# A fused two-block network: the MLP's down-projection by seven products, and the output projection by token tile

## The reference

```python
h = rms_norm(x, norm_mix) * (1 + sc_m) + sh_m
y = fox_mixer(h, ...)              # attention; ends with o @ w_out
x = x + g_m * y
h = rms_norm(x, norm_mlp) * (1 + sc_f) + sh_f
x = x + g_f * (square(relu(h @ w_mlp_in)) @ w_mlp_out)   # 1024 -> 4096 -> 1024
```

## Time and profile before

| | |
|---|---|
| time of the launch, three runs | 3262.44 us median (3258.41 to 3263.48) |
| profiled execution: its time; its span | 3264.19 us; 3262.4 us |
| PE, DVE, ACT busy | 2970.6 (91%), 1293.9 (40%), 679.2 us (21%) |
| down-projection, L922 MATMUL x1024 | 446.0 us |
| output projection, L776 MATMUL x256 | 112.7 us |
| DMA over the span | 305.14 MB, 94 GB/s |

### The profile page before, as it was taken

How to read it: one execution, slowest core, us unless ns; L and a number is a source line. 1 busy time by engine, 2 the same in 40 slices (tenths; PEclk the granted TensorE clock), 3 DMA queues, 4 the chain that set the end, 5 groups by cost and what they waited for, 6 DMA issues and landing times. The chain is left out here.

```text
span 3262.4 us, 51362 instructions
## 1 busy us (share of the span) xinstructions
PE 2970.6 (91%) x20752; PEld 1924.7 (59%) x20752; DVE 1293.9 (40%) x3483; ACT 679.2 (21%) x1552; POOL 261.9 (8%) x343
## 2 busy tenths in 40 slices
PE   3999979988799999999998699999999989799996
PEld 2555546663488544886444377777777745444442
DVE  3222247761355201552001456666666537211115
ACT  2111146650200000000000134444444400111111
POOL 0000011100000000000000022222222200100001
PEclk9999989998899999999998899999999989799998
DMA  4011022211022320123213200000000020599974
GB/s 194 21 39 39 19 84 84 95 64 52 26 78 91 135 78 32 65 91 110 77 45 124 86 16 10 24 15 11 24 9 18 2 113 27 227 353 353 354 274 181
DMA packets 55409, 305.14 MB, mean 94 GB/s; under 512 B 6800, under 2 KB 8336, under 8 KB 39200
## 3 DMA queue, kind: packets, MB, share of 16 engines
q1 hardware_dynamic: 47248, 272.80, 22.8%
q0 software_dynamic: 6912, 25.17, 2.1%
q10 hardware_dynamic: 1040, 4.19, 0.3%
HBM read 269.04 MB, written 33.10 MB: 93 GB/s over the span
## 5 line engine op out<-in xcount | busy, mean ns | idle before, releaser
L922 PE MATMUL mlp_ps<-mlp_w2s,mlp_hid 128*128 128x512 f32 x1024 | 446.0, 599 | 7.4 <-DMA mlp_w2s<-in_w 7.4
L922 PEld LDWEIGHTS mlp_ps<-mlp_w2s,mlp_hid 128*128 128x128 f32 x1024 | 196.9, 193 | 255.3 <-issue 255.2
L328 PE MATMUL qkv_pq<-qkv_wq,h_hT 128*128 128x384 f32 x1024 | 330.5, 487 | 0.0
L1367 PE MATMUL rwkv_ps<-x_xT,rwkv_ws 128*128 128x256 f32 x1152 | 291.9, 391 | 0.0
L328 PEld LDWEIGHTS qkv_pq<-qkv_wq,h_hT 128*128 128x128 f32 x1024 | 194.8, 190 | 135.9 <-issue 0.9
L1367 PEld LDWEIGHTS rwkv_ps<-x_xT,rwkv_ws 128*128 128x128 f32 x1152 | 208.9, 191 | 28.9
L1037 DVE TENSOR_TENSOR mlp_small<-mlp_ps,b_gates 128x512 f32<-128x512 f32 x16 | 11.1, 691 | 421.1 <-PE mlp_ps L922 421.1
L1681 POOL TENSOR_TENSOR rwkv_ML<-rwkv_GM,rwkv_cst 128x256 f32<-128x256 f32 x120 | 99.9, 848 | 474.5 <-DVE rwkv_GM L1737 299.1
L966 ACT COPY mlp_first_copy<-mlp_ps 128x256 f32<-128x256 f32 x32 | 11.9, 372 | 599.7 <-PE mlp_ps L890 599.7
L890 PE MATMUL mlp_ps<-h_hT,mlp_w1s 128*128 128x256 f32 x512 | 122.9, 384 | 6.0 <-DMA mlp_w1s<-in_w 6.0
L1969 PE MATMUL mixr_ps<-mx_w_mix,mx_mixT 128*128 128x512 f32 x256 | 115.3, 606 | 8.7 <-DMA mixr_cnt<-in_counts 8.7
(11 more groups left out here) (382 smaller groups left out, 4593.9 us busy)
## 6 DMA issues: line engine op xcount, KB each, us to landing
mlp_w1s<-in_w SPq DMA_DIRECT2D x32, 1024.0 KB, 4.8
mlp_w2s<-in_w SPq DMA_DIRECT2D x64, 512.0 KB, 3.6
mx_gu<-in_w_gu SPq DMA_DIRECT2D x16, 2048.0 KB, 8.4
mx_w_mix<-in_w_gu SPq DMA_DIRECT2D x16, 2048.0 KB, 8.6
att_wa<-in_w_ada SPq DMA_DIRECT2D x32, 512.0 KB, 3.8
mx_dn<-in_w_d SPq DMA_DIRECT2D x16, 1024.0 KB, 10.3
mx_mixT<-in_w_d SPq DMA_DIRECT2D x16, 1024.0 KB, 10.5
y_rows<-ex_y SPq DMA_DIRECT2D x32, 512.0 KB, 3.0
```

The costliest lines, as they stand in the source:

```text
L328: last = nc.tensor.matmul(pq[:, b, 0:QN], lhsT=hT[:, k, t * P:(t + 1) * P], rhs=wq[:, n, k, :], start=(k == 0), stop=(k == KT - 1))
L922: return nc.tensor.matmul(ps[:, c, :], lhsT=hid[:, f, (c // 2) * P:(c // 2 + 1) * P], rhs=w2s[:, slot(f), (c % 2) * NB:(c % 2 + 1) * NB], ...
L1367: last = nc.tensor.matmul(ps[:, bank, 0:UT], lhsT=ws[:, n, k, :], rhs=xT[:, k, bass.ds(col, UT)], start=(k == 0), stop=(k == KT - 1))
```

## The change

**Output projection.** `stage_modulation_rest` goes, and its work moves into `stage_out`. `w_o` comes in eight DMAs of 512 KB during attention, each into the key columns of a head pair whose scores are done; its columns are laid out in pieces of 128 (512 bytes) for each row. PE makes the first gate, four token tiles (both halves of the width for each), the second gate and the column sums, and then the other four tiles.

**Down-projection.** For each half of the tokens there are two passes over `w2`, each for 256 tokens, with seven banks and seven products a pair of hidden tiles. DVE makes four sums of weights (T, 512 wide) and four of `hid` (S, 128 wide) for each pair, in `hT` columns that are no longer read, for two pairs in turn. ACT copies the seven results of a pass to SBUF, and DVE combines, scales and adds them in 15 steps (`finish`) beside the next pass or the next half's up-projection. `w2s` becomes four slots of two hidden tiles (1 MB), and all of `w2` is loaded four times instead of twice.

```diff
-def stage_modulation_rest(nc, ada_acc, b_ada, cols, modc, gates, ones):
...
@@ stage_attention, SP
+                    sp.wait_ge(maxed, 24 * (p - 1))
                     if p < HEAD_PAIRS:
-                        sp.wait_ge(maxed, 24 * (p - 1))
                         sp.dma_start(frow[:, p % 2, :, :], f_rows[2 * p:2 * p + 2, :].partition_broadcast(P)
                                      ).then_inc(f_in[p % 2], 16)
+                    sp.dma_start(qkv[:, :, cols(1, p - 2)], w_o[p - 2]).then_inc(wo_in, 16)
+                sp.wait_ge(wo_in, 16 * HEAD_PAIRS)
@@ stage_out, PE
+                gate_sums(0)
+                for t in range(TT):
+                    for n in range(2):
+                        m = 2 * t + n
                         if m >= 4:
                             pe.wait_ge(gated, m - 3)
                         for k in range(KT):
+                            last = nc.tensor.matmul(py[:, m % 4, :], lhsT=qkv[:, t, k * P:(k + 1) * P],
+                                                    rhs=qkv[:, k, D + n * NB:D + (n + 1) * NB], start=(k == 0), stop=(k == KT - 1))
                         last.then_inc(mm, 1)
+                    if t == 3:
+                        pe.wait_ge(gate_row, 1)
+                        gate_sums(1)
+                        column_sums(nc, ada_acc[1:3], pmod, ones).then_inc(mm_mod, 1)
@@ stage_mlp, PE: lhsT and rhs of the seven products of a pair, and a pass
+                    lhsT, rhs = {"m1": (raw(0, t1), weight(0, 0)), "m2": (raw(1, t1), weight(1, 0)),
+                                 "m3": (S[:, 3 * P:4 * P], weight(1, 1)), "m4": (raw(1, t2), T[2]),
+                                 "m5": (S[:, 0:P], T[0]), "m6": (S[:, P:2 * P], T[1]),
+                                 "m7": (S[:, 2 * P:3 * P], weight(0, 1))}[name]
...
+                    for i, name in enumerate(PRODUCTS):
...
+                        for j in range(2):
+                            down_product(g, j, name)
+                    for j in range(2, FPAIRS - 2):
+                        for name in PRODUCTS:
+                            down_product(g, j, name)
+                    for name in PRODUCTS:
+                        for j in range(FPAIRS - 2, FPAIRS):
+                            down_product(g, j, name)
@@ stage_mlp, ACT
+                    for g in range(2 * half, 2 * half + 2):
+                        for i in range(7):
+                            act.wait_ge(whole, 7 * g + i + 1)
+                            nc.scalar.copy(copies[g % 2][:, i, :], ps[:, i, :]).then_inc(copied, 1)
@@ stage_mlp, DVE: waits of a pair's sums, and what stands between two pairs
+                    if j >= 2:
+                        pair_done(dve, g, j - 2)
...
+                    pass_sums(2 * half, lambda: None)
+                    rest = finish(2 * half)
                     if half == 0:
+                        turned = tokens_of(1)
+                        pass_sums(1, lambda: (some(rest, 2), some(turned, 1)))
+                        every(sums_of(FPAIRS))
+                    else:
+                        pass_sums(3, lambda: some(rest, 2))
+                    rest = finish(2 * half + 1)
```

More of the change, by code:

```diff
@@ L826, in up_at @@
-        def up_at(j, name):
-            return 7 * j + PRODUCTS.index(name) + 1
-        def part_at(j, name):
-            return 7 * j + PARTS.index(name) + 1
-        def square_at(j, name):
-            return 4 * j + ("c22", "c11", "c21", "c12").index(name) + 1
-        def bank(j, name):
-            return (7 * j + PRODUCTS.index(name)) % 8
-        def slot(f):
-            return (f + 4) % G
+        summed, tokens, made, whole, copied, ended = (
+            s.sem(n) for n in "summed tokens made whole copied ended".split())
@@ new lines, in up_at, with part_at, square_at, bank @@
+        def up_at(n, name):
+            return 7 * n + PRODUCTS.index(name) + 1
+        def part_at(n, name):
+            return 7 * n + PARTS.index(name) + 1
+        def square_at(n, name):
+            return 4 * n + ("c22", "c11", "c21", "c12").index(name) + 1
+        def bank(n, name):
+            return (7 * n + PRODUCTS.index(name)) % 8
+        def slot(j):
+            return (j + 2) % 4
+        def made_order(g):
+            return ([(j, i, x) for i in range(4) for j in range(2) for x in "TS"] +
+                    [(j, i, x) for j in range(2, FPAIRS) for i in range(4) for x in "TS"])
@@ new lines, in pair_done @@
+        def pair_done(eng, g, j):
+            if j == FPAIRS - 1:
+                eng.wait_ge(whole, 7 * g + 7)
+            else:
+                eng.wait_ge(down, (FPAIRS - 1) * g + j + 1)
+        made_at = {}
+        for g in range(PASSES):
+            for key in made_order(g):
+                made_at[(g,) + key] = len(made_at) + 1
+        NEEDS = {"m5": ((0, "T"), (0, "S")), "m6": ((1, "T"), (1, "S")), "m7": ((2, "T"), (2, "S")),
+                 "m4": ((3, "T"),), "m3": ((3, "S"),)}
@@ L845, in pair_weights @@
                     n = half * FPAIRS + j
+                    if half and j < 2:
+                        sp.wait_ge(ended, 15)
                     if n >= 2:
@@ L943, in _ @@
[L943 to L958 removed]
+                    down_pass(2 * half)
@@ L1026, in gather @@
                     dve.wait_ge(squared, square_at(n, "c12"))
-                def take(half, c):
-                    m = half * 8 + c
-                    t, cs = half * 4 + c // 2, slice((c % 2) * NB, (c % 2 + 1) * NB)
-                    if c < 7:
-                        dve.wait_ge(whole, 7 * half + c + 1)
-                    else:
-                        dve.wait_ge(down, (half + 1) * FT)
-                    if m >= 2:
-                        dve.wait_ge(added, m - 1)
-                    nc.vector.tensor_tensor(tmp[:, m % 2, :], ps[:, c, :], gate[:, cs], ALU.mult).then_inc(gated, 1)
-                    dve.wait_ge(gated, m + 1)
-                    nc.vector.tensor_tensor(xres[:, t, cs], xres[:, t, cs], tmp[:, m % 2, :], ALU.add).then_inc(added, 1)
@@ L1043, in _, with some, pass_sums @@
+                def some(steps, count):
+                    for _ in range(count):
+                        next(steps, None)
+                def pass_sums(g, between):
+                    for key in made_order(g):
+                        down_sums(g, *key)
+                        if key[0] >= 2 and key[1:] == (3, "S"):
+                            between()
+                every(zip(tokens_of(0), sums_of(0)))
+                rest = iter(())
                 for half in range(2):
```

267 lines of the change are left out of this document (173 added, 94 removed).

## The result

| | before | after |
|---|---|---|
| time of the launch, median | 3262.78 us (3258.41 to 3263.48, four runs) | 3183.1 us (3179.2 to 3187.32, four runs) |
| ratio, 95% interval | | 0.9759 (0.9742 to 0.9776) |
| profiled execution: its time; its span | 3264.19; 3262.4 us | 3181.23; 3179.4 us |
| PE, DVE, ACT busy | 2970.6, 1293.9, 679.2 us | 2900.8, 1520.5, 696.2 us |
| DMA over the span | 305.14 MB, 94 GB/s | 338.75 MB, 107 GB/s |

A forecast was written before the change was run, and what follows sets the result against it. PE, busy for 91% of the span, was taken to bound the kernel. 68.5 + 16.7 - 1.0 - 1.0 - 3.7 = 79.5 us less gave 3183 us, range 3170 to 3198 us (forecast's own 3175 to 3190).

The forecast's parts named there:

- Products, waits for `w2`, and the clock behind them: Down-projections: 55.0 us less from 448 products instead of 512, 7.4 from waits, 6.1 from slow clock; 68.5 us less.
- rival of the second reading of `w2`: Down-projection: pairs 2 and 3 land 3 us late in each pass, 12 us more, 3195 us; chance 0.03.
- Start of each half: Down-projection, passes 1 and 3: PE waits about 0.5 us each for DVE's first sums; 1.0 us, between 0 and 3.
- DVE's pace: Down-projection: PE waits 1.0 us for DVE's sums, between 0 and 10; as a rival 3193 us, chance 0.07.
- slow steps: Down-projection: each 512-wide sum holds DVE 1.2 us, PE waits 37 us, 3220 us; chance 0.01.
- PE's waits: Down-projection: every semaphore wait costs PE 0.17 us, 65 us in all, 3248 us; chance 0.03.
- The end: End of the down-projection: DVE ends 5.1 us behind PE instead of 1.4; 3.7 us more, between 2 and 7.
- The output projection: PE's restart to the end of the output projection: 16.7 us less, between 10.5 and 18.
- the dip behind the column sums: Output projection: one-column products amid dense ones may make the clock fall; 1.3 us taken, between 0 and 3.1.
- the slow stretch at the start: Output projection: PE starts at half clock as before, costing 2.7 us both before and after the change.
- The loads of `w_o`: Attention: loading `w_o` there delays nothing on the path; 0 us, between 0 and 2.
- The clock as the way to a slower kernel: Down-projection passes: repeated long waits bring half clock; with a quarter of MATMULs slow, 3299 us; chance 0.02.

The follow-up runs named there:

- x3_last4: The kernel before, with PE going bank by bank over the last four hidden tiles instead of eight, products still 512: 3245.07 us, ratio 0.9964.
- x6_dve6: The changed kernel with six more 512-wide additions on DVE for each pair of hidden tiles: 3318.25 us, ratio 1.0175.
- x4_late_wo: The changed kernel with the eight loads of `w_o` issued when the output projection begins instead of during attention: 3201.19 us, ratio 0.982.
- x11_after_2: The changed kernel run once more with nothing altered: 3179.86 us in a single run.

## Why the prediction was right, step by step

- *Products, waits for `w2`, and the clock behind them, 68.5 us.* Right. The two stretches of down-projection lost 67.7 us together, start waits included; `x3_last4` gives 14.0 for waits and clock (forecast 13.5). The rival of the second reading of `w2` falls: no wait for it.
- *Start of each half, 1.0 us.* 0.7: 0.35 us of waiting in each.
- *DVE's pace, 1.0 us.* 0. The size was a little off and the side chosen right: the sums of a pair take 3.2 us (forecast 3.3), the fullest pair 5.75 (forecast 6.0). The added instruction lasts 0.28 us, and the next starts 0.20 or 0.21 us behind it, as the 0.19 of the scalings let expect. By the Trainium skill's figure for fp32 tensor_tensor (VectorE: DVE Perf Modes, "The TRN2 errata") it would be 0.29, an estimate, which is near its duration and not the distance of starts; and the rule that the prediction took from "The DRAIN you can't avoid" does not hold here either, since sums that last 0.69 us are followed by the next after 0.60. The prediction gave it without a limit that the same section states: a next operation that is not held starts earlier. With that limit the section does not speak against the rows, and "slow steps" was a weaker rival than it seemed. The rivals of slow steps and of PE's waits fall: 384 waits on semaphores that were already passed cost nothing that the trace shows.
- *The end, 3.7 us.* 3.6 (5.0 instead of 1.4). The terms of the prediction add to 9.5 - 4.5 = 5.0 as well, where it wrote 5.1.
- *The output projection, 16.7 us.* 18.8 in the profiled execution. Two terms were off there, both of them the clock's: the dip behind the column sums (I took 1.3) did not come, and the slow stretch at the start cost 1.7 us (118.80 against the 117.11 of executions without it) where I took 2.7. Over all executions seen, seven of the new block (mean 119.9 us) and three of the old (137.57, 136.07, 133.80; mean 135.8), it is 15.9. The average is nearer to my 16.7 than the one execution is.
- *The loads of `w_o`, 0 us.* Right as far as can be seen: attention is no longer with them than without, 292.5 against 292.2 us on average, with executions up to 4.8 us apart.
- *Not foreseen.* PE now idles 6.3 us instead of 2.8 before the turning stage, and its 64 MATMULs take 9.7 us instead of 8.6: the clock is 0.50 for 5.2 us behind the restart and not for 3.0. Ten of the eleven executions with the new end take 9.5 to 9.8 us there and one 8.6; the three with the old end take 7.2 to 8.6. So 1.1 us more belong to the price of the end.
- *The clock as the way to a slower kernel.* Not here: no wait in the passes was over 0.4 us. `x6_dve6` shows the mechanism at a price of some 22 us, and that DVE's pace alone, 98.5 us of waits, is enough to turn the gain into a loss.

My sum from the first trace, 79.5 us, agrees with 79.7 of the medians and with 83.0 of the two profiled executions, which differ by clock stretches outside the change as well. That it came within 0.2 us of the medians is chance: the interval of the ratio allows 73 to 84 us, and the errors of the terms (1.3 us too much for the starts and DVE's pace, 1.0 too little for the end) nearly cancel. What stays open is why PE's clock starts low behind attention in some executions and not in others, and why the dip behind the column sums was seen only in executions that began so (`x4_late_wo` among them).

## What to carry to other kernels

Before paying for fewer products, see what the last ones wait for: a loop that needs all of its buffers at once cost 14 us here, in waits and in the slow clock behind them. An engine that feeds PE pair by pair may fill its pace to the brim, since waits of 1.2 us in each pair of 7.45 us cost 1.4 us each and no clock; give it work up to PE's period and no more. Loads into space that is free early belong in the stage before: the same bytes in the same 512-byte pieces, loaded at the start of their own stage, cost 18 us.

## What the runs showed of the hardware that I had not expected

- The granted clock behind one and the same barrier differs between executions of one kernel: in front of the output projection it stayed at 1.00 (`x11_after_2`) or was 0.50 for 3.4 us (the changed kernel).
- 32 MATMULs of one column amid dense ones were followed by some 6.8 us at 0.50 in three of seven executions of the block, with 3.3 or 3.4 us lost in each, and by nothing in the other four.
- SP needed 11.86 us to issue eight loads of 512 KB in 512-byte pieces back to back, 1.5 us each, where beside attention, spaced out, one took 0.55 us.
